# A convolution stage in which GpSimd computes one channel tile beside VectorE, and projections run over four pairs of banks

## The chip, the cores and the metric

The kernel runs on one core of a Trainium2 chip. Its time is the device time of one launch in microseconds (us). Five engines work side by side, each on a queue of its own in program order, and wait for one another by semaphores: TensorE (PE in the profile; PEld is its weight load), VectorE (DVE), ScalarE (ACT), GpSimd (POOL) and SyncE (SP), which here only issues DMA.

## What is computed

One inference step of a decoder with two layers, for a prompt of 512 tokens and 8 x 4 sample tokens: 544 columns in all, with 1024 channels. The change lies in the mixer of the second layer, a Conformer convolution module:

```python
a = h @ conv_w_pw1 + conv_b_pw1
u = a[..., :D_MODEL] * jax.nn.sigmoid(a[..., D_MODEL:])          # gated unit
up = jnp.concatenate([buf, u], axis=1)                            # 30 columns in front
c = depthwise_conv(up, conv_w_dw) + conv_b_dw                     # 31 taps per channel
mu, var = mean(c), mean(square(c - mu))                           # over channels
ln = (c - mu) * rsqrt(var + eps) * conv_ln_g + conv_ln_b
y = silu(ln) @ conv_w_pw2
```

Before it stand the first layer (attention and a gated recurrence) and its retrieval over 16384 single-neuron experts, behind it the retrieval of the second layer; those take most of the time.

## The kernel before

Data lie with channels on the 128 partitions, in eight channel tiles of 128 (`KC = 8`), and with tokens along the free dimension. A weight matrix is streamed as tiles of 128x1024 that are numbered through the whole kernel; `T_PW1 = 302` to 317 are the 16 tiles of the first pointwise projection, in pairs: tile 302 + 2m gives the linear half of channel tile m, the next one the half for its sigmoid. `T_PW2 = 318` to 325 are the second projection.

Each weight tile passes a fixed path. SyncE loads it into a raw buffer (two of them here, `raw_buffer`), once the tile before in that buffer has been split (`s_lo`). ScalarE copies its rounded part into a ring of eight slots (`hi`, L1059, `s_hi`). GpSimd subtracts that from the raw tile (`lo`, L2088, 128x1024, `s_lo`). TensorE multiplies three times, rounded by rounded, rounded by rest, rest by rounded (`proj`, L633 to L646), and counts `s_used`.

The convolution stage, engine by engine:

- TensorE: the projection tiles 0 to 15 go into `PA[t % 2]`, so the linear half of a pair always uses the same pair of PSUM banks, and a tile waits for the gated unit (`s_u`, three counts each) or the sigmoid (`s_sg`) of the pair before (L1005 to L1011). Then the depthwise convolution of channel tiles 6 and 7 (`CONV_PE`) as 31 matmuls each with diagonal matrices (L1018), and the column sums of all eight tiles for the mean (L1027), in the order 0, 1, 2, 3, 6, 7, 4, 5, each behind that tile's `s_cvp`.
- ScalarE (L1418 to L1433): at step i the rounded part of weight tile 306 + i; at odd i the sigmoid of a pair (L1426). Behind step 7 it makes 33 of the 62 diagonals (L1432), behind step 15 the rest as TensorE frees them.
- VectorE (L2036 to L2067): the gated units (`glu`, L2016) and the taps of channel tiles 0 to 5 (`CONV_DVE`). The first tap of a tile is a multiply and add (L2051), the other 30 are multiply with a tensor added (L2054), each waiting for the tap of the same tile before. Two tiles are active at a time and take turns; a tile becomes active once its gated unit has been issued. The gated unit of tile 1 comes after 12 taps (`FIRST_PACE`), each further one after 16 (`PACE`). When the last tile has become active, the taps of the sample tokens are put in (`sample_taps`).
- GpSimd (L2145 to L2151): the subtracts for weight tiles 302 to 317, then a wait for channel tiles 4 and 5 to be done, then the subtracts of the second projection.

Behind the last tap: column sums, centring, squares and their sums, normalisation, and the second projection.

Of the kernel before, what the change touches and what calls it, by code (L numbers as in the profile page):

```python
# [40 lines left out]
CW = 31  # L41
SCALE = HD ** -0.5

CONV_DVE, CONV_PE = (0, 1, 2, 3, 4, 5), (6, 7)
FIRST_PACE, PACE = 12, 16
NDIAG = 33
ND, NDB = 384, 3
DENSE, LONE = (0, 1, 2), (4, 3)
NPART = 15
# [160 lines left out]
def build(nc, xT, stream, utab, vtab, params, consts, mconsts, reset, keysT, kcacheT, vcache, kvcache_n, state_h, convT,  # L210
          yT, kwin_p, vwin_p, hs_p, cb_p, kwin_s, vwin_s, hs_s, cb_s):
    ctx = ExitStack()
    with ctx:
# [146 lines left out]
        with ExitStack() as z:  # L360
            up = sb("up", [P, KC, CW - 1 + NP], F32, z)
            us = sb("us", [P, KC, SB, CW - 1 + ST], F32, z)
            cv = sb("cv", [P, KC, NT], F32, z)
            with ExitStack() as zz:
                diag = sb("diag", [P, NDIAG, P], F32, zz)
            hf_conv = sb("hf_conv", [P, KC, NT], F32, z)
            sg = sb("sg", [P, 2, NT], F32, z)
            wprod = sb("wprod", [P, 2, SB, ST, CW], F32, z)
        sb("arena", [P, 19800])

        psum = [ctx.enter_context(nc.psum_tensor(f"bank{i}", [P, 2, 512], F32)) for i in range(4)]
# [212 lines left out]
        s_u = sem("glu_ready")  # L584
        s_dg = sem("tap_diagonal_ready")
        s_dgu = sem("tap_diagonal_used")
        s_cvp = [sem(f"conv_done{k}") for k in range(KC)]
        s_cvs = sem("sample_conv_done")
        s_ms = sem("mean_sum_done")
# [16 lines left out]
        def y_bank(k):  # L606

            return (PB[1][:, 1, :], PA[0][:, 0, :], PA[0][:, 1, :], PA[1][:, 0, :], PA[1][:, 1, :],
                    PB[0][:, 0, :], PB[0][:, 1, :], PB[1][:, 0, :])[k]

        SUMS = [PA[0], PB[0], PA[0], PB[0]]
        HF = [hf_mix, hf_peer, hf_conv, hf_peer]
# [8 lines left out]
        def _(pe):  # L621
# [16 lines left out]
            def proj(t, first=False, event=None):  # L638

                pe.wait_ge(s_lo, t + 1)  # L640
                for k in range(KC):
                    if first:
                        pe.wait_ge(s_hl, 8 * H_EVENT[event] + k + 1)
                    for i, (w, h) in enumerate(((ring_hi, hh), (ring_hi, hl), (ring_lo, hh))):
                        for a in range(2):
                            m = T.matmul(PA[t % 2][:, a, 0:HALF], w[:, ring_slot(t), k * P:(k + 1) * P],  # L646
                                         h[:, k, a * HALF:(a + 1) * HALF],
                                         start=(k == 0 and i == 0), stop=(k == KC - 1 and i == 2))
                m.then_inc(s_used, 1)
# [353 lines left out]
            experts(0)  # L1003
            norm(2)
            for i in range(16):  # L1005
                if i >= 2:
                    if i % 2 == 0:
                        pe.wait_ge(s_u, 3 * (i // 2))
                    else:
                        pe.wait_ge(s_sg, i // 2)  # L1010
                proj(T_PW1 + i, i == 0, "n2")  # L1011
            for n, k in enumerate(CONV_PE):

# [36 lines left out]
        def _(act):  # L1050
# [367 lines left out]
            for i in range(16):  # L1418
                if T_PW1 + LOOK + i < T_PW2 + 2:
                    hi(T_PW1 + LOOK + i)  # L1420
                if i % 2:
                    m = i // 2
                    act.wait_ge(s_used, T_PW1 + i + 1)
                    if m >= 2:
                        act.wait_ge(s_u, 3 * (m - 1))
                    A.activation(tok2(sg[:, m % 2, :]), both(PA[(T_PW1 + i) % 2]), ACT.Sigmoid,  # L1426
                                 bias=pc("b1", 8 + m)).then_inc(s_sg, 1)
                if i == 7 or i == 15:
                    for d in (range(0, NDIAG) if i == 7 else range(NDIAG, CW * len(CONV_PE))):
                        if d >= NDIAG:  # L1430
                            act.wait_ge(s_dgu, d - NDIAG + 1)
                        A.activation(diag[:, d % NDIAG, :], ident, ACT.Copy,  # L1432
                                     scale=pc("wdw", CW * CONV_PE[d // CW] + d % CW)).then_inc(s_dg, 1)  # L1433
# [35 lines left out]
        def _(dve):  # L1469
# [536 lines left out]
            def glu(m):  # L2006
                dve.wait_ge(s_used, T_PW1 + 2 * m + 1)
                dve.wait_ge(s_sg, m + 1)
                pa = PA[T_PW1 % 2]
                for o, i0, i1 in ((up[:, m, CW - 1:CW - 1 + HALF], pa[:, 0, 0:HALF], sg[:, m % 2, 0:HALF]),  # L2010
                                  (up[:, m, CW - 1 + HALF:CW - 1 + NP], pa[:, 1, 0:NP - HALF],
                                   sg[:, m % 2, HALF:NP]),
                                  (us[:, m, :, CW - 1:CW - 1 + ST],
                                   pa[:, 1, NP - HALF:HALF].rearrange("p (b t) -> p b t", b=SB),
                                   sg[:, m % 2, NP:NT].rearrange("p (b t) -> p b t", b=SB))):
                    V.scalar_tensor_tensor(out=o, in0=i0, scalar=pc("b1", m), in1=i1,  # L2016
                                           op0=ALU.add, op1=ALU.mult).then_inc(s_u, 1)
# [66 lines left out]
        @block.gpsimd  # L2084
        def _(pool):
            def lo(t, slot, buf):
                pool.wait_ge(s_hi, t + 1)
                nc.gpsimd.tensor_tensor(ring_lo[:, slot, :], raw[buf][:], ring_hi[:, slot, :].bitcast(F32),  # L2088
                                        ALU.subtract).then_inc(s_lo, 1)

            def lo_run(a, b):

                for t in range(a, b):
                    lo(t, ring_slot(t), raw_buffer(t))

            def gather_rows(l):

                for i in range(N_ROWS):
                    g = N_ROWS * l + i
                    b, is_v, j = row_of(i)  # L2100
                    if i == 0:
                        pool.wait_ge(s_gi, 2 * (l + 1))
                        pool.wait_ge(s_gm, (ND // 8) * (l + 1))
                        pool.wait_ge(s_gs, (ND // 8) * (l + 1))
                    if i >= ROW_SLOTS:
                        pool.wait_ge(s_rd, g - ROW_SLOTS + 1)
                    nc.gpsimd.indirect_dma_start(  # L2107
                        out=rows[:, g % ROW_SLOTS, :], out_offset=None, in_=vtab if is_v else utab,
                        in_offset=bass.IndirectOffsetOnAxis(ap=gidx[b][:, j:j + 1], axis=0))\
                        .then_inc(s_row[g % ROW_SLOTS], 16)  # L2110

            lo_run(0, 10)
            pool.wait_ge(s_qr, 5)
            pool.dma_start(resm, reset).then_inc(s_reset, 16)
            lo_run(10, 20)
            pool.wait_ge(s_o, 16)
            pool.dma_start(kcat[:, :, 0:WIN], kcacheT).then_inc(s_dload, 16)
            pool.dma_start(vcat[:, :, :], vcache).then_inc(s_dload, 16)
            lo_run(20, N_IN)
            pool.wait_ge(s_do, 1)  # L2120
            def load_state(b):
                pool.dma_start(Ssm[b % 4], state_h[b].rearrange("h k v -> k h v")).then_inc(s_sl[b % 4], 16)

            for b in range(4):
                load_state(b)
            lo(T_OUT, ring_slot(T_OUT), raw_buffer(T_OUT))
            for b in range(SB):
                pool.wait_ge(s_S, 2 + NPC + b)
                if b + 4 < SB:
                    pool.wait_ge(s_oc, NPC + b + 1)  # L2130
                    load_state(b + 4)
                pool.dma_start(hs_s[b].rearrange("h k v -> k h v"), Snew[b % 4]).then_inc(s_so[b % 4], 16)
            pool.dma_start(hs_p.rearrange("h k v -> k h v"), Sb[NPC % 2]).then_inc(s_hsp, 16)
            for i in range(4):
                pool.wait_ge(s_so[i], 16 * (SB // 4))
            pool.wait_ge(s_hsp, 16)
            lo_run(T_OUT + 1, T_OUT + N_OUT)
            pool.wait_ge(s_res, 1)
            pool.dma_start(keys[:, :, :], keysT[0]).then_inc(s_keys, 16)
            lo_run(T_WQ[0], T_WQ[0] + N_WQ + 3)  # L2140
            gather_rows(0)
            pool.wait_ge(s_wl, NKEY)
            pool.wait_ge(s_yt, KC + 1)
            pool.wait_ge(s_used, T_EXP[0] + N_EXP)
            lo_run(T_PW1, T_PW1 + LOOK)  # L2145
            for k in range(KC):
                pool.dma_start(us[:, k, :, 0:CW - 1], convT[k * P:(k + 1) * P]).then_inc(s_conv, 16)
            lo_run(T_PW1 + LOOK, T_PW2)
            for m in CONV_DVE[-2:]:
                pool.wait_ge(s_cvp[m], 1)  # L2150
            lo_run(T_PW2, T_PW2 + KC)  # L2151
            pool.wait_ge(s_res, 9)
            pool.wait_ge(s_out, 16 * 15)
            pool.dma_start(keys[:, :, :], keysT[1]).then_inc(s_keys, 16)
            lo_run(T_WQ[1], T_WQ[1] + N_WQ + 3)
            gather_rows(1)
# [118 lines left out]
```

## Time and profile before

| what | value |
|---|---|
| median of 3 runs | 3400.09 us (3398.16 to 3400.13) |
| the profiled execution | 3398.86 us |
| its span in the trace | 3397.1 us |
| busy: TensorE matmul, VectorE, ScalarE, GpSimd | 94%, 81%, 41%, 35% of the span |
| the convolution stage (first gated unit to last tap) | 1776 to 1957 us |

Times in the trace count from the start of the span. A row of a timeline gives start, duration, engine, line, operation, output and inputs, shapes, the number of instructions merged into it, and in brackets the idle time before it with what ended it. Neighbouring instructions of one form are merged into one row, whose duration goes from the first start to the last end; rows of one engine can overlap by the pipeline's depth. Busy shares are averages over stages with different limits, so a stage is read by itself.

### The profile page before, as it was taken

How to read it: one execution, taken by the hardware profiler on the slowest of the kernel's cores; microseconds unless marked ns; L12 is line 12 of the kernel's file. 1: busy time of each engine (PE TensorE's matmuls, PEld its weight loads, DVE VectorE, ACT ScalarE, POOL GpSimd, SP SyncE). 2: the span in 40 equal slices, each digit the busy share in tenths (PEclk: the TensorE clock that was granted, in tenths of full speed). 3: DMA queues.
4: the chain of work that ended last, by engine and by line, in shares of the span. 5: the costliest groups of instructions: out<-in, count | busy, mean ns of one | idle time of the engine just before them, and what ended most of it. 6: DMA issues, size and time to landing. Idle time of an engine off the chain costs nothing.

```text
span 3397.1 us, 48906 instructions
## 1 busy us (share of the span) xinstructions
PE 3188.6 (94%) x18193; PEld 2910.0 (86%) x18193; DVE 2744.3 (81%) x5402; ACT 1393.5 (41%) x2305; POOL 1192.3 (35%) x766
## 2 busy tenths in 40 slices
PE   8899997998999999999988879889989999999999
PEld 7788897998888888888878478889978888888888
DVE  6546389889788888888869937998878888888887
ACT  4653215777333333333332132277843333333332
POOL 2122321000455455555542033100015555555554
PEclk9887998999999999999999989999989999999999
DMA  3111322554999999999941332245569999999997
GB/s 124 49 63 60 91 66 87 202 193 143 373 376 369 358 369 359 361 367 358 370 142 56 12 82 65 66 160 202 205 225 380 367 367 359 370 357 365 367 358 268
DMA packets 425212, 807.82 MB, mean 238 GB/s; under 512 B 234176, under 2 KB 259328, under 8 KB 421504
## 3 DMA queue, kind: packets, MB, share of 16 engines
q1 hardware_dynamic: 318496, 453.12, 39.7%
q0 software_dynamic: 94560, 344.45, 27.3%
q10 hardware_dynamic: 11920, 7.12, 1.4%
q8 instruction: 145, 2.38, 0.3%
q14 instruction: 91, 0.75, 0.1%
HBM read 729.52 MB, written 76.08 MB: 237 GB/s over the span
## 4 chain that ended last, share of the span: by engine, by line
PE 76%; DVE 20%; ACT 2%; DMA 1%; issue 1%; ACTq 0%; SPq 0%; DVEq 0%
PE bank L905 31%; PE bank L893 27%; PE bank L646 11%; DVE cv L2054 3%; PE bank L876 3%; DVE oh L1699 2%; DVE oh L1694 2%; DMA units_ahead<-ga 1%; DVE pick L1665 1%; DVE eidx L1681 1%; DVE pick L1674 1%; DVE si L1530 1%; PE bank L788 1%; DVE ring L1708 1%; DVE sc L1532 1%
## 5 line engine op out<-in xcount | busy, mean ns | idle before, releaser
L893 PE MATMUL bank<-hh,ring 128*128 128x384 f32 x4096 | 1098.3, 341 | 34.5 <-DVE sc L1532 23.5
L905 PE MATMUL bank<-ring,wh 128*128 128x512 f32 x3072 | 828.3, 391 | 0.0
L2107 POOL DMA_INDIRECT rows<-in_utab,gidx x320 | 449.9, 1406 | 1066.5 <-ACT stage L1191 635.7
L1708 DVE TENSOR_TENSOR ring<-raw,ring 128x1024 fp32r<-128x1024 f32 x506 | 616.4, 1221 | 238.4 <-ACT ring L1059 237.7
L893 PEld LDWEIGHTS bank<-hh,ring 128*128 128x128 f32 x4096 | 751.8, 190 | 42.5 <-issue 36.4
L1059 ACT ACTIVATE ring<-raw 128x1024 fp32r<-128x1024 f32 x598 | 621.3, 1052 | 175.0 <-PE bank L893 100.0
L893 PE MATMUL bank<-hl,ring 128*128 128x384 f32 x2048 | 691.4, 338 | 0.0
L905 PEld LDWEIGHTS bank<-ring,wh 128*128 128x128 f32 x3072 | 574.4, 188 | 111.1
L2107 POOL DMA_INDIRECT rows<-in_vtab,gidx x320 | 492.1, 1538 | 367.4 <-DVE acc L1748 314.9
L646 PE MATMUL bank<-hh,ring 128*128 128x272 f32 x2752 | 497.8, 300 | 62.6 <-DVE hl L1486 46.8
L1153 ACT ACTIVATE ga<-bank 128x384 f32<-128x384 f32 x256 | 124.3, 486 | 998.2 <-PE bank L893 983.4
L646 PEld LDWEIGHTS bank<-hh,ring 128*128 128x128 f32 x2752 | 410.5, 196 | 77.8 <-issue 52.4
L905 PE MATMUL bank<-ring,wl 128*128 128x512 f32 x1536 | 473.1, 389 | 0.0
L2088 POOL TENSOR_TENSOR ring<-raw,ring 128x1024 fp32r<-128x1024 f32 x92 | 227.1, 2476 | 676.0 <-ACT ring L1059 545.5
L1748 DVE SCALAR_TENSOR_TENSOR acc<-rows,wv,acc 128x1024 f32<-128x1024 f32 x316 | 404.5, 1280 | 12.3 <-DVE acc L1748 0.5
L893 PEld LDWEIGHTS bank<-hl,ring 128*128 128x128 f32 x2048 | 390.1, 190 | 6.1
L1740 DVE CUSTOM_DVE_ANT_0 rows<-rows,htok 128x1024 f32<-128x1024 f32 x320 | 381.6, 1218 | 0.2 <-DMA rows<-in_utab,gidx 0.2
L905 PEld LDWEIGHTS bank<-ring,wl 128*128 128x128 f32 x1536 | 288.3, 188 | 64.1
L646 PE MATMUL bank<-hl,ring 128*128 128x272 f32 x1376 | 293.6, 295 | 0.0
L876 PE MATMUL bank<-oh 128*128 128x128 f32 x1536 | 202.4, 289 | 60.9 <-DVE oh L1699 53.8
L876 PEld LDWEIGHTS bank<-oh 128*128 128x128 f32 x1536 | 193.7, 203 | 68.2 <-DVE oh L1699 59.8
L646 PEld LDWEIGHTS bank<-hl,ring 128*128 128x128 f32 x1376 | 226.2, 196 | 0.0
(316 smaller groups left out, 2913.9 us busy)
## 6 DMA issues: line engine op xcount, KB each, us to landing
raw<-in_stream SPq DMA_DIRECT2D x342, 512.0 KB, 5.6
raw<-in_vtab SPq DMA_DIRECT2D x256, 512.0 KB, 7.9
gate_matrix<-stage SPq DMA_DIRECT2D x24, 2048.0 KB, 11.0
gt<-gate_matrix SPq DMA_DIRECT2D x256, 192.0 KB, 9.7
units_ahead<-ga SPq DMA_DIRECT2D x96, 192.0 KB, 4.2
gv<-units_ahead SPq DMA_DIRECT2D x96, 192.0 KB, 8.9
rows<-in_utab,gidx POOLq DMA_INDIRECT x320, 8.1
rows<-in_vtab,gidx POOLq DMA_INDIRECT x320, 7.9
```

The lines of the kernel that those rows point to most:

```text
L646: m = T.matmul(PA[t % 2][:, a, 0:HALF], w[:, ring_slot(t), k * P:(k + 1) * P], h[:, k, a * HALF:(a + 1) * HALF], start=(k == 0 and i == 0) ...
L876: m = T.matmul(PA[e % 2][:, i // 4, (i % 4) * P:(i % 4 + 1) * P], oh2[:, e % 2, i, :], oh1[:, e % 2, i, :], start=True, stop=True)
L893: m = T.matmul(PB[1][:, (e + 1) % 2, 0:ND], w[:, ring_slot(t), k * P:(k + 1) * P], h[:, k, 0:ND], start=(k == 0 and i == 0), stop=(k == KC ...
L905: m = T.matmul(psum[c][:, a, :], w[:, v_n % WSLOT, c * P:(c + 1) * P], v[:, ring_slot(t), 512 * a:512 * a + 512], start=(v_n == 0 and i == ...
L1059: A.activation(ring_hi[:, ring_slot(t), :], raw[b][:], ACT.Copy).then_inc(s_hi, 1)
L1153: A.activation(ga[:, e % ASLOT, :], PB[1][:, (e + 1) % 2, 0:ND], ACT.Gelu).then_inc(s_ga, 1)
L1708: V.tensor_tensor(ring_lo[:, ring_slot(t), :], raw[raw_buffer(t)][:], ring_hi[:, ring_slot(t), :].bitcast(F32), ALU.subtract).then_inc(s_l ...
L1740: V.tensor_tensor_reduce(out=rows[:, slot, :], in0=rows[:, slot, :], in1=htok[b][:, :], scale=1.0, scalar=0.0, op0=ALU.mult, op1=ALU.add, ...
L1748: V.scalar_tensor_tensor(out=acc[b][:, :], in0=rows[:, slot, :], scalar=wv[b][:, j:j + 1], in1=acc[b][:, :], op0=ALU.mult, op1=ALU.add).th ...
L2054: tap = V.scalar_tensor_tensor(out=cv[:, m, 0:NP], in0=up[:, m, i:i + NP], scalar=w, in1=cv[:, m, 0:NP], op0=ALU.mult, op1=ALU.add)
L2088: nc.gpsimd.tensor_tensor(ring_lo[:, slot, :], raw[buf][:], ring_hi[:, slot, :].bitcast(F32), ALU.subtract).then_inc(s_lo, 1)
L2107: nc.gpsimd.indirect_dma_start(out=rows[:, g % ROW_SLOTS, :], out_offset=None, in_=vtab if is_v else utab, in_offset=bass.IndirectOffsetOn ...
```

## The change

One channel tile of the convolution, tile 1, moves from VectorE to GpSimd. There a tap is two instructions on 128x512: a product of the shifted input with the tap's weight, into one of two buffers (`tapped`), and a sum into `cv`. Products run one ahead of the sums, and both wait for earlier ones by semaphores of their own. The first eight tap steps are put between the subtracts of weight tiles 310 to 317; the first of them waits for the gated unit of tile 1. The rest follow in a row.

The projection pairs alternate between the banks `PB` and `PA`, and TensorE waits for the gated unit and the sigmoid two pairs back. A gated unit comes every 13 taps, still after 12 for the first. The first 33 diagonals are made in sevens behind the sigmoids of steps 1, 3, 5, 7 and 9.

```diff
-CONV_DVE, CONV_PE = (0, 1, 2, 3, 4, 5), (6, 7)
-FIRST_PACE, PACE = 12, 16
-NDIAG = 33
+CONV_DVE, CONV_PE, CONV_POOL = (0, 2, 3, 4, 5), (6, 7), 1
+FIRST_PACE, PACE = 12, 13
+NDIAG, DIAG_AT = 33, 7
+POOL_FROM = 4
...
+            tapped = sb("tapped", [P, 2, NP], F32, z)
...
+        def pw1_bank(t):
+
+            m, i = divmod(t - T_PW1, 2)
+            return (PA if m % 2 else PB)[i]
+
+        def proj_bank(t):
+
+            return pw1_bank(t) if T_PW1 <= t < T_PW2 else PA[t % 2]
...
             for i in range(16):
-                if i >= 2:
+                if i >= 4:
                     if i % 2 == 0:
-                        pe.wait_ge(s_u, 3 * (i // 2))
+                        pe.wait_ge(s_u, 3 * (i // 2 - 1))
                     else:
-                        pe.wait_ge(s_sg, i // 2)
+                        pe.wait_ge(s_sg, i // 2 - 1)
                 proj(T_PW1 + i, i == 0, "n2")
...
-                if i == 7 or i == 15:
-                    for d in (range(0, NDIAG) if i == 7 else range(NDIAG, CW * len(CONV_PE))):
+                if i % 2 and i < 10 or i == 15:
+                    d0 = DIAG_AT * (i // 2)
+                    for d in (range(d0, min(d0 + DIAG_AT, NDIAG)) if i < 15 else range(NDIAG, CW * len(CONV_PE))):
...
-            lo_run(T_PW1 + LOOK, T_PW2)
+            def tap_product(i):
+
+                w = pc("wdw", CW * CONV_POOL + i)
+                if i >= 3:
+                    pool.wait_ge(s_tsum, i - 2)
+                if i == 0:
+                    nc.gpsimd.tensor_scalar(cv[:, CONV_POOL, 0:NP], up[:, CONV_POOL, 0:NP], w,
+                                            pc("bdw", CONV_POOL), ALU.mult, ALU.add).then_inc(s_tap, 1)
+                else:
+                    nc.gpsimd.tensor_scalar(tapped[:, i % 2, :], up[:, CONV_POOL, i:i + NP], w, None, ALU.mult)\
+                        .then_inc(s_tap, 1)
+
+            def tap_sum(i):
+
+                pool.wait_ge(s_tap, i + 1)
+                if i >= 2:
+                    pool.wait_ge(s_tsum, i - 1)
+                m = nc.gpsimd.tensor_tensor(cv[:, CONV_POOL, 0:NP], cv[:, CONV_POOL, 0:NP], tapped[:, i % 2, :],
+                                            ALU.add)
+                m.then_inc(s_tsum if i < CW - 1 else s_cvp[CONV_POOL], 1)
+
+            def tap(i):
+
+                if i < CW:
+                    tap_product(i)
+                if 2 <= i <= CW:
+                    tap_sum(i - 1)
+
+            n_tap = 0
+            for t in range(T_PW1 + LOOK, T_PW2):
+                lo(t, ring_slot(t), raw_buffer(t))
+                if t >= T_PW1 + LOOK + POOL_FROM:
+                    if n_tap == 0:
+                        pool.wait_ge(s_u, 3 * (CONV_POOL + 1))
+                    tap(n_tap)
+                    n_tap += 1
+            for i in range(n_tap, CW + 1):
+                tap(i)
             for m in CONV_DVE[-2:]:
                 pool.wait_ge(s_cvp[m], 1)
             lo_run(T_PW2, T_PW2 + KC)
```

The left-out lines put `proj_bank` and `pw1_bank` in place of `PA[...]` in `proj`, in the sigmoid and in the gated unit, and declare the two semaphores.

## Rows read from the trace of the kernel before

**Rows 1.** Windows of the stage: length, busy us (instructions) per engine, PEclk, DMA share, GB/s
```profile
1776.00:1884.00 108.00, 92.70 (x677) 90.37 (x678) 96.54 (x132) 27.03 (x55) 26.97 (x10) 0.95 0.16 50
1884.00:1957.00 73.00, 59.83 (x149) 28.43 (x148) 71.54 (x100) 12.58 (x30) 0.39 (x1) 0.91 0.44 15
```
**Rows 2.** The chain of waits: start us, us, what; its shares from 1922 to 1957
```profile
1823.20 12.34 PE bank L646 x96
...
by line: DVE cv L2054 96.2%; PE bank L1027 2.3%; DVE cv L2051 1.3%; DVE cv L2033 1.2%; issue 1.0%
...
1923.18 23.86 DVE cv L2054 x36
...
1947.82 0.03 issue
1947.85 0.76 DVE cv L2054
```
**Rows 3.** Waits from 1776 to 1957: who for whom, total us, times, longest
```profile
POOL ring L2088 <- DVE cv L2054: 110.0, 1, 110.0
...
DVE up L2016 <- ACT sg L1426: 18.3, 5, 7.9
...
PE bank L646 <- DVE us L2016: 15.7, 7, 3.2
```
**Rows 4.** VectorE's groups of instructions in that window: busy us, mean ns, idle
```profile
L2054 DVE SCALAR_TENSOR_TENSOR cv<-up,par,cv 128x512 f32<-128x512 f32 x180 | 135.0, 814 | 1.2
...
L2051 DVE TENSOR_SCALAR cv<-up,par 128x512 f32<-128x512 f32 x6 | 7.3, 1218 | 0.0
```
**Rows 5.** Timeline of VectorE, taps and first taps
```profile
1777.52 2.52 DVE L2051 TENSOR_SCALAR cv<-up,par 128x512 f32<-128x512 f32 x1
1780.08 10.64 DVE L2054 SCALAR_TENSOR_TENSOR cv<-up,par,cv 128x512 f32<-128x512 f32 x11
...
1791.80 2.79 DVE L2054 SCALAR_TENSOR_TENSOR cv<-up,par,cv 128x512 f32<-128x512 f32 x1
1794.51 2.62 DVE L2051 TENSOR_SCALAR cv<-up,par 128x512 f32<-128x512 f32 x1
...
1807.27 13.98 DVE L2054 SCALAR_TENSOR_TENSOR cv<-up,par,cv 128x512 f32<-128x512 f32 x16
...
1837.34 15.28 DVE L2054 SCALAR_TENSOR_TENSOR cv<-up,par,cv 128x512 f32<-128x512 f32 x15
...
1840.09 1.41 DVE L2054 SCALAR_TENSOR_TENSOR cv<-up,par,cv 128x512 f32<-128x512 f32 x2
...
1841.42 5.71 DVE L2054 SCALAR_TENSOR_TENSOR cv<-up,par,cv 128x512 f32<-128x512 f32 x2
...
1853.93 10.68 DVE L2054 SCALAR_TENSOR_TENSOR cv<-up,par,cv 128x512 f32<-128x512 f32 x16
...
1922.64 0.54 DVE L2051 TENSOR_SCALAR cv<-up,par 128x512 f32<-128x512 f32 x1
```
**Rows 6.** Timeline of GpSimd, subtracts of weight tiles
```profile
1791.65 5.19 POOL L2088 TENSOR_TENSOR ring<-raw,ring 128x1024 fp32r<-128x1024 f32 x2 [9.35 <-ACT ring L1059]
1805.93 5.48 POOL L2088 TENSOR_TENSOR ring<-raw,ring 128x1024 fp32r<-128x1024 f32 x2 [9.09 <-ACT ring L1059]
...
1840.80 5.78 POOL L2088 TENSOR_TENSOR ring<-raw,ring 128x1024 fp32r<-128x1024 f32 x2 [2.50 <-ACT ring L1059]
...
1995.94 2.38 POOL L2088 TENSOR_TENSOR ring<-raw,ring 128x1024 fp32r<-128x1024 f32 x1 [2.40 <-ACT ring L1059]
```
**Rows 7.** GpSimd's groups over the whole span, the shortest kind
```profile
L2259 POOL MEMSET const-float32-0.0<- 128x1 f32 x1 | 0.1, 98 | 0.2 <-issue 0.2
```
**Rows 8.** Timeline of TensorE: the convolution of tiles 6 and 7, the last column sums
```profile
1882.04 53.40 PE L1018 MATMUL bank<-up,diag 128*128 128x512 f32 x124
...
1956.53 2.18 PE L1027 MATMUL bank<-cv,con 128*128 128x272 f32 x4 [7.93 <-DVE cv L2054]
```
**Rows 9.** Timeline of ScalarE, the first diagonals
```profile
1821.91 9.76 ACT L1432 ACTIVATE diag<-con,par 128x128 f32<-128x128 f32 x33
```

## What the change should do to the time

> **What bounds the kernel now.** The change touches only the convolution stage, from 1776 to 1957 us of the span, so I read that stretch alone, in the order of the groups of rows. The windows by engine come first [rows 1]: VectorE is busy for 96.5 of 108 us and then for 71.5 of 73 us; TensorE comes near it (92.7 and 59.8 us), so the share alone does not say which of them sets the end; ScalarE is at a quarter or less, and GpSimd works 27.0 us and then next to nothing. The chain of waits over the last 35 us [rows 2] is VectorE's tap line for 96.2%: 36 taps of two channel tiles in turn take 23.86 us, 0.664 us each, and a tap of one tile alone, which waits for its own predecessor, takes 0.76 us and 0.03 us of issue, 0.787 us. TensorE's last column sums, four matmuls, stand idle 7.93 us until the last tap is done [rows 8]; behind them come the norm and the second projection. So the time at which VectorE finishes its last tap sets the end of the stage, and every microsecond there is one of the kernel. The waits [rows 3] show what else is in that time: VectorE waits 18.3 us for the sigmoid in five places; the longest, 7.9 us, stands before any product exists and stays, so 10.4 us can be won. TensorE's 15.7 us of waiting for gated units cost only through those 10.4 us. GpSimd's idle 110.0 us is what the change wants to fill.
>
> The last reading decides the case: what GpSimd's work does to a tap. Against its groups [rows 4] a tap (L2054) has a mean of 814 ns and a first tap (L2051) 1218 ns, although undisturbed ones take 0.66 to 0.76 us [rows 2] and 0.54 us [rows 5]. The excess lies where GpSimd runs its subtract of the weight tiles (L2088) [rows 5, 6]. At 1791.65 GpSimd starts two subtracts; the tap that starts at 1791.80 lasts 2.79 us, and the first tap of the next tile behind it 2.62 us. At 1840.80 it runs two more: the two taps from 1841.42 take 5.71 us, where the two before them took 1.41 us. One tap gets through per GpSimd instruction, and the GpSimd instruction waits for that tap in turn (two subtracts take 5.78 us there, one alone 2.38 us at 1995.94, so a turn of VectorE is (5.78 - 4.76) / 2 = 0.5 us). These are the taps of the kernel itself, reading two tiles of SBUF; they and GpSimd take turns by whole instructions. Price of one turn: (5.71 - 1.41) / 2 = 2.15 us per subtract of 2.38 us. A GpSimd instruction costs VectorE its own duration less 0.23 us.
>
> **The change part by part.** Costs are in time of VectorE, against the profiled execution of 3398.86 us (span 3397.10 and 1.76 around it); the median of the runs is 1.2 us higher.
>
> Taps taken away: 31 of 186, 31 x 0.664 [rows 2] = 20.6 us won.
>
> Banks in four pairs: a projection pair now waits for the gated unit two pairs back, so TensorE runs ahead and each sigmoid is ready before its turn: at most the 10.4 us above are won [rows 3]. I take all of it, since below the gated units come later than TensorE needs to keep ahead.
>
> GpSimd's taps: 31 products of one input and 30 sums of two inputs, each 128x512. No row has either. The nearest is the 128x1024 subtract, two inputs, 2.38 us [rows 6]; a GpSimd instruction of one column lasts 0.10 us [rows 7]. Half of 2.28 us and that fixed part give 1.24 us for a sum; its ends are 1.19 us (no fixed part) and 1.4 us (0.4 us fixed); I take 1.25. A product reads one tile where the sum reads two: no less than VectorE's own first tap of that shape, 0.54 us [rows 5], no more than the sum; I take 0.95 us, between half a sum and a whole one. The price by the turns: 31 x (0.95 - 0.23) + 30 x (1.25 - 0.23) = 22.3 + 30.6 = 52.9 us lost, with ends of 31 x 0.31 + 30 x 0.96 = 38.4 and 31 x 1.02 + 30 x 1.17 = 66.7 us. The Trainium skill, GPSIMD Engine Reference, section 4.1 Engine selection, calls GpSimd's one-input operations roughly line-rate, and section 3.1 gives 769 ns for 512 elements of a tight loop; with that estimate the products would cost 31 x 0.54 = 16.7 us, 5.6 us less. No run here shows it yet.
>
> Cover: a gated unit reads PSUM and one SBUF tile. When two subtracts started at 1805.93 it ran beside them, and the 16 taps behind took 13.98 us against 10.68 us undisturbed [rows 5, 6]: 3.3 us instead of 4.3, so a gated unit hides about 1.0 us. Six of them (the third to the eighth) fall into GpSimd's chain: 6.0 us less lost. If this cover is missing the sum grows by those 6 us.
>
> The ten subtracts cost VectorE today (2.52 - 0.54) + (10.64 - 11 x 0.787) at 1777, (2.79 - 0.76) + (2.62 - 0.54) at 1791, 3.3 at 1807 and 15.28 - 10.0 at 1837: 16.7 us [rows 5]. Part of them lies under waits for sigmoids and gated units; with those waits gone or used by the new instructions all ten cost 2.15 us, 21.5 us: 4.8 us lost.
>
> One tile alone: with tile 1 on GpSimd, the second active tile is tile 2, which needs the third gated unit. Tile 0 runs alone for 25 taps instead of 12, 13 x (0.787 - 0.664) = 1.6 us lost; at the end the last tile is alone for 7 taps instead of 12, 0.6 won. Net 1.0 us lost.
>
> Nothing for the rest, with its cover. Pace of 13 instead of 16: it only fixes the place of a gated unit among taps. Diagonals in sevens: 33 of them, 9.76 us [rows 9], stood in front of weight tiles on ScalarE; spread out, each seven delays two tiles by 7 / 33 of that, 2.1 us, beside a TensorE that waits for VectorE. GpSimd's own queue: behind each new instruction stand the subtracts of weight tiles 310 to 317, for which TensorE, and the SyncE loads that wait for their raw buffers, wait; one product and one sum with their turns are about 3.2 us against the 12.34 us in which TensorE uses two tiles [rows 2]. GpSimd's chain from about 1792: 31 x 0.95 + 30 x 1.25 + 8 x 2.38 = 86 us, and some 69 turns of a tap at 0.5 us, 34.5 us: it ends near 1913, 65 us before VectorE, so the sums' wait for tile 1 and the later subtracts (which wait for tiles 4 and 5, as now) cost nothing. TensorE's two tiles of the convolution take 53.4 us for 62 taps of two matmul records each [rows 8], 0.86 us a tap. By the same chain the eighth gated unit moves from 1884 to about 1917, and TensorE's second tile ends 27 us later near 1945, over 30 us before VectorE.
>
> Sum: 52.9 - 6.0 + 4.8 + 1.0 - 20.6 - 10.4 = 21.7 us lost: 3398.86 + 21.7 = 3420.6, and as a median of runs 3422 us. With the ends of the two unknown prices: +7.2 to +35.5 us, 3407 to 3436 us. The last tap moves from 1956.5 to about 1978.
>
> **The rivals.** (a) Only GpSimd's two-input instructions take turns with VectorE; the products run beside the taps. Then 22.3 us fall away: 21.7 - 22.3 = -0.6 us, 3400 us, no change. For it: every GpSimd instruction that the trace shows to stop a tap has two inputs. Against it: it is the VectorE side that differs, the gated unit with one SBUF input passes, while taps and also the one-input first tap stop (2.52 and 2.62 against 0.54 us) [rows 5]. The Trainium skill, GPSIMD Engine Reference, section 8 Key points, puts the contention on VectorE's instructions with two SBUF inputs or in a two-port mode and exempts no GpSimd instruction; the 2.52 us row agrees on VectorE's side, and by that rule (a) has no place.
>
> (b) Faster. The products run beside the taps and the sums are short for their width. The place is the 30 sums, the price 30 x (duration - 0.23); with free products the kernel gains over 6.8 us only when a sum lasts under 1.04 us: at 0.95 us it would be 21.6 - 6.0 + 4.8 + 1.0 - 20.6 - 10.4 = -9.6 us, 3391 us. Against it: half a subtract is 1.19 us.
>
> (c) The change does more harm: a product with a scalar per partition lasts as long as a sum or longer. At 1.4 us each the price is 61 x 1.17 = 71.4 us instead of 52.9, +40.2, 3440 us. From the rows only the missing second input speaks against it.
>
> (d) GpSimd's chain becomes the bound: it would have to be 65 us longer, a product of 3 us; the rows give no reason. I leave it inside (c).
>
> **How the numbers follow.** Forecast 0.62, (a) 0.18, (b) 0.06, (c) 0.14. A measurement of this kernel tells about 0.2% from no change, 6.8 us. Forecast and (c) are slower by more than that, except for the low end of the forecast's own range (+7.2, at the border), so 0.03 of it goes to no change, with 0.15 of (a). (a) can come out a little better or worse than the bound: 0.02 to faster, 0.01 to slower. Faster 0.08, same 0.18, slower 0.74. The range goes from (a), 3400, to (c), 3440: it leaves out (b) and the tails of (a) and (c).
>
> **What would show it.** Right: GpSimd's 128x512 rows near 0.95 and 1.25 us, longer where a tap runs; VectorE's tap mean over 1.0 us, with taps of about a GpSimd instruction plus 0.5 us until about 1913 and 0.66 to 0.76 us after; no wait for a sigmoid after the first; gated units later though paced by fewer taps; last tap near 1978. Wrong: taps of 0.74 us beside a running product (a); GpSimd's sums near 1 us (b); GpSimd still at its taps when VectorE ends (d).

## The result: slower, by less than half of what was forecast

| kernel | median of runs | ratio to the kernel before, 95% interval | profiled execution, span |
|---|---|---|---|
| before (in the same runs) | 3399.79 us | | 3397.1 us |
| changed | 3409.85 us | 1.0028 (1.0018 to 1.0039) | 3403.7 us |

One execution of the changed kernel (3986.9 us) and one of the later run with a shared tile (3428.5 us) had a lower granted clock, 0.74 and 0.90 against 0.96 and 0.97 in the others, and the ratios leave them out.

The kernel became 10.1 us slower; 22 us were forecast. The stage itself answers for it: from the first gated unit to TensorE's last column sums it took 1956.53 - 1776.45 = 180.1 us before and takes 1963.44 - 1773.70 = 189.7 us now, 9.7 us more. (The two profiled executions differ by only 6.6 us, because the changed one came to the stage 2.75 us earlier; behind the last column sums both need 1440 us.) The first gated units, before and now:

```profile
1776.45 0.88 DVE L2016 SCALAR_TENSOR_TENSOR up<-bank,par,sg 128x272 f32<-128x272 f32 x2 [7.93 <-ACT sg L1426]
```
```profile
1773.70 0.88 DVE L2030 SCALAR_TENSOR_TENSOR up<-bank,par,sg 128x272 f32<-128x272 f32 x2 [7.94 <-ACT sg L1439]
```

Line numbers of the changed kernel are some 14 higher: taps L2068, first taps L2065, gated units L2030, GpSimd's subtract L2102, its product L2171 (the first one L2168), its sum L2179.

The windows of the stage, columns as in [rows 1]:

```profile
1774.00:1902.00 128.00, 113.52 (x720) 97.98 (x720) 126.89 (x124) 36.88 (x79) 113.00 (x62) 0.95 0.14 42
1902.00:1964.00 62.00, 37.45 (x97) 18.63 (x96) 60.79 (x76) 1.99 (x4) 16.26 (x11) 0.81 0.53 18
```

VectorE is now busy for 126.89 of 128 us, the gaps before sigmoids are gone but for the first, and GpSimd's 27 us have become 113 us. The groups of instructions, answering to [rows 4]:

```profile
L2068 DVE SCALAR_TENSOR_TENSOR cv<-up,par,cv 128x512 f32<-128x512 f32 x150 | 152.0, 1069 | 1.3
L2171 POOL TENSOR_SCALAR tapped<-up,par 128x512 f32<-128x512 f32 x30 | 57.4, 1914 | 2.3
L2179 POOL TENSOR_TENSOR cv<-cv,tapped 128x512 f32<-128x512 f32 x30 | 43.8, 1459 | 0.1
L2041 DVE TENSOR_TENSOR wprod<-us,par 128x496 f32<-128x496 f32 x16 | 14.6, 975 | 0.2
```

There are 30 taps less, and they take 17 us more in all: a mean of 1069 ns instead of 814. The sample tokens' products (L2041), whose first rows now fall beside the end of GpSimd's chain, went from 670 ns to 975. Of GpSimd's own instructions the one-input product is the longer one, 1.91 us, against 1.46 us for the two-input sum. That is where the forecast broke, and the timelines of the steady stretch show how. GpSimd first, one tap of the convolution, then VectorE's three taps beside it in two overlapping windows:

```profile
1848.52 1.89 POOL L2171 TENSOR_SCALAR tapped<-up,par 128x512 f32<-128x512 f32 x1
1850.38 1.51 POOL L2179 TENSOR_TENSOR cv<-cv,tapped 128x512 f32<-128x512 f32 x1
1851.99 1.88 POOL L2171 TENSOR_SCALAR tapped<-up,par 128x512 f32<-128x512 f32 x1
```
```profile
1848.90 1.84 DVE L2068 SCALAR_TENSOR_TENSOR cv<-up,par,cv 128x512 f32<-128x512 f32 x2
...
1849.99 2.44 DVE L2068 SCALAR_TENSOR_TENSOR cv<-up,par,cv 128x512 f32<-128x512 f32 x2
```

Two undisturbed taps take 1.41 us [rows 5]. The pair from 1848.90, which meets the product, takes 1.84 us: 0.43 us lost, and the second of them runs free while the product goes on until 1850.41. The pair from 1849.99, its second tap meeting the sum, takes 2.44 us: 1.03 us lost. So three taps, not two, pass in one product and sum, and a product of 1.89 us costs VectorE 0.43 us.

TensorE's projection now waits for VectorE's gated units three times instead of seven, and the last column sums, answering to [rows 8], stand idle for 3.99 us:

```profile
PE bank L659 <- DVE us L2030: 11.4, 3, 6.3
```
```profile
1963.44 2.18 PE L1040 MATMUL bank<-cv,con 128*128 128x272 f32 x4 [3.99 <-DVE cv L2068]
```

**The books of the stage.** For each tap, first tap and sample product I took its duration over the undisturbed one (0.745, 0.54 and 0.67 us) and put the excess down to the GpSimd instruction that ended inside it, or, where none ended inside it, to the product that was running beside it (a product outlasts the tap that it holds up):

| excess on VectorE | subtracts | products | sums |
|---|---|---|---|
| before | 16.5 us (9 of 10) | | |
| changed | 19.6 us (10) | 11.2 us (27 of 31) | 25.5 us (27 of 30) |

Those not counted were hidden under gated units or reductions. 19.6 + 11.2 + 25.5 - 16.5 = 39.8 us lost, less 20.6 us of taps and 10.4 us of waits, plus the 1.0 us of one tile alone, which is the prediction's term and was not measured, is +9.8 us; the stage measured +9.7.

### The profile page after: what moved, and what is told of

Its sections match the earlier page's. It is cut to its first block, busy times and chain, and to the rows that moved or that the text cites. A ratio compares the mean times of both kernels' runs of the same rounds, so it can differ in the third digit from the quotient of the medians.

```text
span 3403.7 us, 48962 instructions
## 1 busy us (share of the span) xinstructions
PE 3183.3 (94%) x18193; PEld 2906.5 (85%) x18193; DVE 2764.6 (81%) x5371; ACT 1394.0 (41%) x2305; POOL 1294.6 (38%) x827
## 3 DMA queue, kind: packets, MB, share of 16 engines
q8 instruction: 145, 2.38, 0.3%
## 4 chain that ended last, share of the span: by engine, by line
PE 73%; DVE 23%; ACT 1%; DMA 1%; issue 1%; ACTq 0%; SPq 0%; DVEq 0%
PE bank L918 31%; PE bank L906 26%; PE bank L659 9%; DVE cv L2068 4%; PE bank L889 2%; DVE oh L1713 2%; DVE oh L1708 2%; DMA units_ahead<-ga 1%; DVE pick L1679 1%; DVE eidx L1695 1%; DVE pick L1688 1%; DVE ring L1722 1%; DVE si L1544 1%; PE bank L801 1%; DVE sc L1546 1%
## 5 line engine op out<-in xcount | busy, mean ns | idle before, releaser
L2102 POOL TENSOR_TENSOR ring<-raw,ring 128x1024 fp32r<-128x1024 f32 x92 | 227.9, 2483 | 580.5 <-ACT ring L1072 514.9
```

## The experiments

The theory that went into them: VectorE's tap time sets the end of the stage; a GpSimd product costs a tap 0.43 us and a sum 1.03 us, whatever they last; the banks win the sigmoid's waits. The rivals: the prediction's prices (0.72 us for a product, or its duration less 0.23 us), products that cost nothing, and banks worth nothing.

### Banks, pace and diagonals alone

```diff
-CONV_DVE, CONV_PE, CONV_POOL = (0, 2, 3, 4, 5), (6, 7), 1
+CONV_DVE, CONV_PE, CONV_POOL = (0, 1, 2, 3, 4, 5), (6, 7), 1
...
-            n_tap = 0
-            for t in range(T_PW1 + LOOK, T_PW2):
...
+            lo_run(T_PW1 + LOOK, T_PW2)
```

> The four pairs of banks, the pace of 13 and the diagonals in sevens alone; all six channel tiles stay on VectorE and GpSimd only makes its subtracts. If the waits for the sigmoid are worth what the trace of the kernel before shows (10.4 us), the last tap comes about 170 us behind the first gated unit instead of 180 us, and the kernel takes about 3389 us. If the subtracts that then fall on taps give back what the prediction counted (4.8 us), it takes about 3394 us. If banks and pace are worth nothing, 3400 us.

Measured: 3388.48 us, ratio 0.9970 (0.9961 to 0.9980), faster than both kernels. The waits, the first gated unit and the last column sums:

```profile
DVE up L2030 <- ACT sg L1439: 7.9, 1, 7.9
```
```profile
1775.51 0.88 DVE L2030 SCALAR_TENSOR_TENSOR up<-bank,par,sg 128x272 f32<-128x272 f32 x2 [7.93 <-ACT sg L1439]
```
```profile
1936.07 2.18 PE L1040 MATMUL bank<-cv,con 128*128 128x272 f32 x4 [17.25 <-DVE cv L2068]
1946.18 2.18 PE L1040 MATMUL bank<-cv,con 128*128 128x272 f32 x4 [7.93 <-DVE cv L2068]
```

Of five waits for a sigmoid only the first is left, and the stage is 1946.18 - 1775.51 = 170.7 us long. This half of the change is worth 10 us; against it, GpSimd's tile costs about 20. Whether the banks, the pace or the diagonals win the 10 us was not parted. TensorE stands idle for 25 us (17.25 + 7.93) in front of its last column sums.

### The whole change with the old banks

```diff
-            return (PA if m % 2 else PB)[i]
+            return PA[i]
...
-                if i >= 4:
+                if i >= 2:
...
-                        pe.wait_ge(s_u, 3 * (i // 2 - 1))
+                        pe.wait_ge(s_u, 3 * (i // 2))
...
-                        pe.wait_ge(s_sg, i // 2 - 1)
+                        pe.wait_ge(s_sg, i // 2)
```

> The whole change, but with the projection pairs in one pair of banks and TensorE waiting for the pair just before, as in the kernel before. Theory: with GpSimd's taps beside it VectorE needs 15.2 to 20.2 us from one gated unit to the next, and TensorE and ScalarE need only 14.3 us for the next pair, so VectorE would wait for no sigmoid with the old banks either: the same time as the whole change, 3410 us. Rival, the prediction's sum, in which the banks are worth 10.4 us on their own: 3420 us.

Measured: 3409.43 us, ratio 1.0030 (1.0018 to 1.0042), the time of the whole change.

```profile
DVE up L2030 <- ACT sg L1439: 8.8, 2, 7.9
```

VectorE waits for only one sigmoid beyond the first, 0.9 us, where the kernel before waits for four, 10.4 us. With GpSimd's chain beside it VectorE is so slow between gated units that TensorE keeps ahead with either arrangement. The 10.4 us that the prediction booked for the banks are real, but in the whole change the slowness of VectorE would have removed those waits without them.

### Sums without products, products without sums

```diff
-                pool.wait_ge(s_tap, i + 1)
+                pool.wait_ge(s_tap, min(i, 2) + 1)
...
-                if i < CW:
+                if i < 3:
                     tap_product(i)
```

> The whole change without 28 of GpSimd's 31 products: the sums are all made, from the second and third product again and again, so channel tile 1 is not the convolution. Theory: a product holds a tap up for 0.43 us, so 28 of them are worth some 10 us (a few lie under gated units): 3400 us. Rival, the prediction's price of 0.72 us each: 20 us, 3390 us. Rival, products run beside the taps: 3410 us, as with the whole change.

Measured: 3396.22 us, ratio 0.9996 (0.9987 to 1.0005), 0.0032 x 3400 = 11 us below the whole change. In the steady stretch each sum meets one tap:

```profile
1859.78 8.29 POOL L2179 TENSOR_TENSOR cv<-cv,tapped 128x512 f32<-128x512 f32 x5
```
```profile
1858.42 10.20 DVE L2068 SCALAR_TENSOR_TENSOR cv<-up,par,cv 128x512 f32<-128x512 f32 x6
```

Six taps in 10.20 us are 1.70 us each, 1.03 us over the undisturbed spacing, and the books give 26.6 us for 28 sums. The price of a sum does not hang on the product in front of it.

```diff
-                    pool.wait_ge(s_tsum, i - 2)
+                    pool.wait_ge(s_tap, i - 1)
...
-                if i >= 2:
-                    pool.wait_ge(s_tsum, i - 1)
...
-                if 2 <= i <= CW:
+                if i == CW:
                     tap_sum(i - 1)
```

> The whole change without 29 of GpSimd's 30 sums: all products are made, and one sum, so channel tile 1 is not the convolution. Theory: a sum holds a tap up for 1.03 us and three of 30 are hidden, so 29 are worth 24 to 25 us: 3385 us. By the same theory the taps beside a product keep their 0.43 us more. Rival: a GpSimd instruction costs its own duration less 0.23 us, and a product that lasts 1.9 us costs more than a sum: without the sums 3395 us or more.

Measured: 3381.99 us, ratio 0.9955 (0.9941 to 0.9968), 0.0073 x 3400 = 25 us below the whole change, as the theory had it.

```profile
1849.03 7.49 POOL L2171 TENSOR_SCALAR tapped<-up,par 128x512 f32<-128x512 f32 x4
```
```profile
1849.30 1.84 DVE L2068 SCALAR_TENSOR_TENSOR cv<-up,par,cv 128x512 f32<-128x512 f32 x2
...
1852.01 4.18 DVE L2068 SCALAR_TENSOR_TENSOR cv<-up,par,cv 128x512 f32<-128x512 f32 x5
```

Products follow one another without a gap here, 1.87 us each in the mean of these four, and VectorE still loses only 0.43 us to each: two taps take 1.84 us. If a product shut VectorE out for its duration, one tap would pass per product.

### What makes a product cheap: its inputs or its length

```diff
-                    nc.gpsimd.tensor_scalar(tapped[:, i % 2, :], up[:, CONV_POOL, i:i + NP], w, None, ALU.mult)\
-                        .then_inc(s_tap, 1)
+                    nc.gpsimd.tensor_tensor(tapped[:, i % 2, :], up[:, CONV_POOL, i:i + NP],
+                                            w.to_broadcast([P, NP]), ALU.mult).then_inc(s_tap, 1)
```

> The whole change, but 30 products read the tap's weight as a second tensor (one column repeated 512 times) instead of as a scalar per partition. Theory: what a tap loses is the time for which the GpSimd instruction streams its inputs, 0.43 us with one input and 1.03 us with two; 30 products cost 0.6 us more each, 18 us less the few under gated units: 3424 to 3428 us. Rival: a product costs what it does because it is a product or because it is short of waits, whatever its inputs: 3410 us.

Measured: 3423.80 us, ratio 1.0066 (1.0054 to 1.0078).

```profile
L2171 POOL TENSOR_TENSOR tapped<-up,par 128x512 f32<-128x512 f32 x30 | 41.9, 1397 | 1.8
```

The products became shorter, 1.40 us instead of 1.91, and the kernel 13 us slower (0.0038 x 3400). The books give 20.9 us to 28 products, 0.75 us each, and 29.4 us to the sums, of which fewer are hidden now. So a product with a second input is dearer, but it costs 0.75 us and not the 1.03 us of a sum. The operation changed with the input (TENSOR_TENSOR for TENSOR_SCALAR), and the run does not part the two. The second input is one column repeated; with a whole tensor there it was not tried.

```diff
-                    nc.gpsimd.tensor_scalar(tapped[:, i % 2, :], up[:, CONV_POOL, i:i + NP], w, None, ALU.mult)\
-                        .then_inc(s_tap, 1)
+                    nc.gpsimd.tensor_scalar(tapped[:, i % 2, :], up[:, CONV_POOL, i:i + NP], w, 0.0,
+                                            ALU.mult, ALU.add).then_inc(s_tap, 1)
```

> The whole change, but 30 products are a multiply and an add of zero, the form of the first product, which lasted 1.20 us where the others last 1.9 us. Theory: the rest of a product's duration holds no tap up, so products get shorter (about 1.2 us), taps beside them lose 0.43 us as before, and the time stays at 3410 us. Rival, the prediction's rule that a GpSimd instruction costs its duration less 0.23 us: 0.7 us less for each of 30, about 3389 us.

Measured: 3411.66 us, ratio 1.0037 (1.0023 to 1.0050), not to be told from the whole change.

```profile
L2171 POOL TENSOR_SCALAR tapped<-up,par 128x512 f32<-128x512 f32 x30 | 30.9, 1031 | 2.3
```

The products shrank by 0.88 us each, 26 us in all, and nothing came of it: the books give 12.0 us to 29 of them. The steady stretch shows it too:

```profile
1851.14 1.02 POOL L2171 TENSOR_SCALAR tapped<-up,par 128x512 f32<-128x512 f32 x1
1852.12 1.71 POOL L2179 TENSOR_TENSOR cv<-cv,tapped 128x512 f32<-128x512 f32 x1
1853.93 1.01 POOL L2171 TENSOR_SCALAR tapped<-up,par 128x512 f32<-128x512 f32 x1
```
```profile
1850.79 11.98 DVE L2068 SCALAR_TENSOR_TENSOR cv<-up,par,cv 128x512 f32<-128x512 f32 x9
```

A product and a sum now take 2.79 us (1851.14 to 1853.93), and two taps pass in that time, one held up by each: 2.79 - 2 x 0.664 = 1.46 us are lost. In the whole change they take 3.47 us (1848.52 to 1851.99) and three taps pass: 1.48 us lost. The duration of a GpSimd instruction is not its price.

### GpSimd's chain beside an idle VectorE

```diff
-                if t >= T_PW1 + LOOK + POOL_FROM:
...
-                    tap(n_tap)
-                    n_tap += 1
+            pool.wait_ge(s_u, 3 * (CONV_POOL + 1))
+            for m in CONV_DVE[-2:]:
+                pool.wait_ge(s_cvp[m], 1)
             for i in range(n_tap, CW + 1):
                 tap(i)
-            for m in CONV_DVE[-2:]:
-                pool.wait_ge(s_cvp[m], 1)
```

> The whole change, but GpSimd begins its taps only when VectorE has finished channel tiles 4 and 5, so that the chain runs beside an idle VectorE. Theory: VectorE's last tap comes about 153 us behind the first gated unit (189.7 us less the 36.7 us that taps lose to products and sums now); products alone last about 1.57 us and sums 1.33 us, so the chain takes about 89 us more, and seven column sums follow: about 3466 us. Rival: a product's 1.9 us are mostly waiting for VectorE and alone it lasts 0.6 us: about 3436 us.

Measured, once and without an interval: 3456.7 us. GpSimd's timeline, the first product, then a later product and sum:

```profile
1923.19 0.76 POOL L2168 TENSOR_SCALAR cv<-up,par 128x512 f32<-128x512 f32 x1 [96.87 <-DVE cv L2068]
...
1928.38 1.56 POOL L2171 TENSOR_SCALAR tapped<-up,par 128x512 f32<-128x512 f32 x1
1929.91 1.26 POOL L2179 TENSOR_TENSOR cv<-cv,tapped 128x512 f32<-128x512 f32 x1
```

Alone, a sum lasts 1.26 us and a product 1.56 us: most of the product's length is its own and not a wait for VectorE, so the rival with 0.6 us falls. VectorE's last 53 taps:

```profile
1886.89 36.07 DVE L2068 SCALAR_TENSOR_TENSOR cv<-up,par,cv 128x512 f32<-128x512 f32 x53
```

They end at 1923.0, 152.9 us behind the first gated unit at 1770.1, where 153 was expected: without products and sums the books close. The chain took 87 us (1923.2 to 2010.5). The kernel's time is 9 us under the expected one; 4 us of that lie in front of the stage, which began at 1770.1 instead of 1773.7 in this execution, and another 4 us behind the last column sums, from which it is 1436.3 us to the end instead of 1440.2; why was not followed up.

### A version that beats both

TensorE's idle 25 us with banks alone are room for half a channel tile. Its first 16 taps go to TensorE, in front of tiles 6 and 7; ScalarE copies the sum from PSUM, and VectorE adds the other 15.

```diff
-CONV_DVE, CONV_PE, CONV_POOL = (0, 2, 3, 4, 5), (6, 7), 1
+CONV_DVE, CONV_PE, CONV_POOL = (0, 1, 2, 3, 4, 5), (6, 7), 1
...
+SHARED, N_SHARED = 5, 16
+TAPS_PE = [(SHARED, i) for i in range(N_SHARED)] + [(k, i) for k in CONV_PE for i in range(CW)]
...
-            order = (0, 1, 2, 3, 6, 7, 4, 5)
+            order = (0, 1, 2, 3, 6, 7, 5, 4)
...
+                        if d - NDIAG + 1 == N_SHARED:
+                            A.activation(cv[:, SHARED, 0:NP], PB[1][:, 1, 0:NP], ACT.Identity, bias=pc("bdw", SHARED))\
+                                .then_inc(s_part, 1)
...
-                        dve.wait_ge(s_v, at[m])
+                        if m in at:
+                            dve.wait_ge(s_v, at[m])
+                        else:
+                            dve.wait_ge(s_part, 1)
...
+            lo_run(T_PW1 + LOOK, T_PW2)
```

> Banks, pace and diagonals of the change, all subtracts but no taps on GpSimd, and the first 16 taps of channel tile 5 on TensorE in front of tiles 6 and 7; VectorE adds the other 15 to what ScalarE copies out of PSUM. Theory: VectorE's tap time sets the end, TensorE is idle for 25 us in front of the last column sums with banks alone, and 16 taps less are 16 x 0.664 = 10.6 us: about 3378 us. Rival: TensorE's 13.8 us more push its own convolution and column sums behind VectorE: 3384 us or more.

Measured: 3381.94 us, ratio 0.9946 (0.9937 to 0.9955). TensorE, then ScalarE, then VectorE's centring of the eight tiles:

```profile
1858.74 67.13 PE L1034 MATMUL bank<-up,diag 128*128 128x512 f32 x156
1926.70 5.74 PE L1043 MATMUL bank<-cv,con 128*128 128x272 f32 x24 [0.82 <-issue]
...
1935.74 1.89 PE L1043 MATMUL bank<-cv,con 128*128 128x272 f32 x4 [1.84 <-DVE cv L2077]
```
```profile
1926.39 16.68 ACTq L1462 DMA_DIRECT2D out_cb_s<-us  x8
1943.12 4.48 ACT L1465 ACTIVATE hf_conv<-cv 128x544 f32<-128x544 f32 x8 [16.52 <-DVE cv L2095]
```
```profile
1938.43 7.01 DVE L2095 TENSOR_TENSOR cv<-cv,sg 128x544 f32<-128x544 f32 x8
```

TensorE's longer convolution is done in time, and its last column sums come 10.3 us earlier behind the first gated unit than with banks alone. But 3 us are given back behind them: from the last column sums to the second projection it is 29.4 us, and 26.3 with banks alone. The transfers of the convolution state wait for TensorE's convolution, which is done at 1925.9 now and was at 1912.3 with banks alone, where they lay under VectorE's taps; now they hold ScalarE until 1943.1, while the first tile was centred by 1941.0. (The first tile takes 2.57 us to centre and the others 0.71 each, because a GpSimd subtract of the second projection runs beside it. The kernel before has the same, 2.33 us; with GpSimd's chain behind the taps, where no subtract falls on it, the first tile takes 0.73 us.) The last run takes the transfers off ScalarE's queue:

```diff
-            act.dma_start(cb_p.rearrange("(k p) n -> p k n", p=P), up[:, :, NP:NP + CW - 1]).then_inc(s_out, 16)
-            for k in range(KC):
-                act.dma_start(cb_s[k * P:(k + 1) * P], us[:, k, :, ST:ST + CW - 1]).then_inc(s_out, 16)
...
+            pool.dma_start(cb_p.rearrange("(k p) n -> p k n", p=P), up[:, :, NP:NP + CW - 1]).then_inc(s_cout, 16)
+            for k in range(KC):
+                pool.dma_start(cb_s[k * P:(k + 1) * P], us[:, k, :, ST:ST + CW - 1]).then_inc(s_cout, 16)
```

> The kernel with the shared tile 5, but the nine output transfers of the convolution state are issued by GpSimd, which is idle there, instead of by ScalarE. In the run with the shared tile ScalarE issued them until 1943.1 us and only then began the squares, 4 us after VectorE had centred the first tile. Theory: those 4 us come out, 3378 us. Rival: GpSimd's issue of transfers holds up VectorE's last taps, or is in front of its subtracts for the second projection, and eats the gain: 3382 us or more.

Measured: 3377.92 us, ratio 0.9939 (0.9925 to 0.9952). GpSimd issues them in 7.01 us, far ahead of its next subtract:

```profile
1866.93 7.01 POOL L2201 DMA_DIRECT2D out_cb_s<-us  x8
1938.60 4.64 POOL L2108 TENSOR_TENSOR ring<-raw,ring 128x1024 fp32r<-128x1024 f32 x2 [64.65 <-DVE cv L2074]
```

The interval overlaps that of the run before, so the medians alone do not settle this last step. In the traces the way from the first gated unit to the second projection is 187.1 us against 189.8, 2.7 us shorter and not the expected 4, which counted the first tile as centred by 1939. The last column sums come 160.4 us behind the first gated unit in both, so issuing the transfers on GpSimd held no tap up.

## Why the prediction was wrong in size

**What bounds the stage: right.** VectorE's taps set the end before and after; every run moved with them but the one that put GpSimd's chain behind them.

**One failing term: the price of a product.** The prediction said "A GpSimd instruction costs VectorE its own duration less 0.23 us", read from subtracts and taps that take turns by whole instructions, and priced 31 products at 0.95 - 0.23 = 0.72 us, 22.3 us. They cost 0.43 us each, 31 x 0.43 = 13.3 us, of which 11.2 us are seen and the rest lies under gated units and reductions. The rule holds for the instruction that it was read from and for the sum, which has two inputs as well; it is false for the product with one input. Both its parts fail: the products last 1.9 us and not 0.95, and yet cost 0.43 us. Their first 0.4 us fall beside the end of a tap, one tap waits, and the next one passes while the product still runs. The two errors partly cancel, and that is luck: the rule takes an instruction's length without a tap beside it, as the subtract's 2.38 us, and with the product's 1.56 us it would have given 31 x 1.33 = 41 us, so that the forecast would have missed by far more. Why only part of a product holds a tap up, no run shows; that the part does not hang on the product's length is shown. Rival (a), products beside the taps at no price, was the other end; the truth lies between it and the forecast, at 0.43 of 0.72 us. A price between the two ends should have had a chance of its own.

| term | forecast | measured |
|---|---|---|
| 31 taps taken away | -20.6 us | fits: from banks alone to the chain behind the taps the last tap comes 17.7 us earlier (152.9 us behind the first gated unit, not 170.6); 20.6 less 1.0 for one tile alone and 1.9 for subtracts (19.7 against 17.8 in the books) is 17.7 |
| waits for the sigmoid | -10.4 us | gone; but gone with the old banks too |
| 31 products | 22.3 us | 13.3 us at 0.43 us each |
| 30 sums | 30.6 us | 30.9 us at 1.03 us each |
| cover of products and sums, by gated units and reductions | -6.0 us | -7.5 us (44.2 less the 36.7 us of the books) |
| subtracts with less cover | 4.8 us | 3.1 us |
| one tile alone | 1.0 us | not measured by itself |

**The sum: right.** 1.25 us were assumed for its length, alone it lasts 1.26; 1.02 us for its price, measured 1.03.

**The pages.** GPSIMD Engine Reference of the Trainium skill, section 4.1 Engine selection, has one-input operations at roughly line rate and section 3.1 the 769 ns for 512 elements of a tight loop. The first product, a multiply with an add, agrees: 0.76 us alone. The other thirty, a multiply without the add, took 1.56 us alone, about twice that, and for them the measurement decides. Section 8 Key points puts the contention on VectorE's instruction and exempts none of GpSimd's; the traces agree that products are not exempt, at 0.43 us for each.

**No cost elsewhere: right.** GpSimd's chain ended at 1918, VectorE at 1963; TensorE's convolution (its end at 1931) and ScalarE's diagonals stayed under the taps, and behind the last column sums the kernel takes 1440.2 us, against 1440.5 before.

## What to carry to other kernels

An engine's idle time is no free room when its instructions shut the busy engine out: compare what one moved instruction takes from the bound engine with what that engine would have spent on it. Here a tap of 0.66 us was swapped for 0.43 + 1.03 us of waiting. And a lost microsecond is read from the disturbed engine's rows, not from the length of the instruction that disturbs it. When a change has a part that helps and a part that hurts, run them apart; here the helpful half alone was worth 10 us, and beside the harmful one its banks were worth nothing.

## What the hardware showed that was not expected

- A one-input GpSimd product of 128x512 that lasts 1.9 us holds a VectorE tap up for 0.43 us; with a repeated column as second input it lasts 1.4 us and holds it up for 0.75 us; a two-input sum of 1.5 us holds it up for 1.03 us, about half of the 2.0 to 2.15 us of the subtract with twice the columns.
- On GpSimd a multiply with an add of zero is shorter than the multiply without it: 1.03 us against 1.91 us beside VectorE (0.76 against 1.56 us alone, the shorter one in the first product only, where the bias is added).
- A gated unit, which reads PSUM and one SBUF tile on VectorE, ran undisturbed beside all of them (0.86 us).
